# Even attention of a two-block kernel: three projection chunks change places, eight more attention units run beside the chunks, and products of the output projection stand between the last units

## What is computed

```python
proj = h @ w_in                       # 1024 x 3080: qa ka va | qb kb vb | forget gates
# differential attention, 4 heads of 2 maps each, chunk mask and ALiBi
s_a = qa . ka * scale - slope * dist  ;  p_a = softmax(s_a)
o_a = (p_a[0] - lam * p_a[1]) @ va    ;  o_a = rms_norm(o_a) * subln_g * 0.8
# forgetting attention, 8 heads, causal
s_b = qb . kb * scale + cq - cum_f    ;  o_b = softmax(s_b) @ vb
mix = concat(o_a, o_b) @ w_out        # 1024 x 1024
h = layer_norm(ALPHA * h + mix)       # then the feed-forward part
```

## Time and profile before

| | |
|---|---|
| median of 3 runs | 1156.41 us (1154.87 to 2162.7) |
| the profiled execution | 1158.03 us, span 1156.2 us |
| TensorE busy, mean granted clock | 1117.0 us (97%), 0.982 |
| VectorE, ScalarE, GpSimd busy | 778.5, 623.9, 332.9 us |
| HBM | 153 GB/s over the span |

### The profile page before, as it was taken

How to read it: one execution, slowest core, us unless ns; L and a number is a source line. 1 busy time by engine, 2 the same in 40 slices (tenths; PEclk the granted TensorE clock), 3 DMA queues, 4 the chain that set the end, 5 groups by cost and what they waited for, 6 DMA issues and landing times.

```text
span 1156.2 us, 24136 instructions
## 1 busy us (share of the span) xinstructions
PE 1117.0 (97%) x8917; PEld 1063.4 (92%) x8917; DVE 778.5 (67%) x1404; ACT 623.9 (54%) x1194; POOL 332.9 (29%) x371
## 2 busy tenths in 40 slices
PE   6998989999988999999999999999999999999997
PEld 6976989999988888779999999999979999999996
DVE  5766578887467777736888555495556567887454
ACT  5657555556445646754665543474335645665343
POOL 3002323334201101125466312100013334666130
PEclk9999999999999999959999999999999999999999
DMA  6573436675555533204555554655422655555651
GB/s 195 135 207 111 111 104 187 184 201 164 168 194 196 182 96 94 91 1 147 182 170 166 178 178 163 212 193 182 145 73 91 202 182 182 183 181 181 203 182 53
DMA packets 202489, 180.61 MB, mean 156 GB/s; under 512 B 6800, under 2 KB 200755, under 8 KB 202163
## 3 DMA queue, kind: packets, MB, share of 16 engines
q1 hardware_dynamic: 201907, 175.74, 48.8%
q0 software_dynamic: 512, 3.94, 0.9%
HBM read 176.28 MB, written 1.05 MB: 153 GB/s over the span
## 4 chain that ended last, share of the span: by engine, by line
PE 84%; DVE 5%; ACT 4%; issue 2%; DMA 2%; POOL 2%; SPq 0%; ACTq 0%; DVEq 0%; POOLq 0%
PE ps L1925 24%; PE ps L1926 24%; PE ps L1927 24%; DVE wlo L1297 2%; PE ps L2338 2%; PE ps L2468 2%; ACT whi L759 1%; PE ps L2083 1%; POOL acc L589 1%; DMA raw<-even_w_in 1%; PE ps L2295 1%; PE ps L2320 1%; PE ps L2446 1%; PE ps L2294 1%; DVE h L1534 1%
## 5 line engine op out<-in xcount | busy, mean ns | idle before, releaser
L1297 DVE TENSOR_TENSOR wlo<-raw,whi 128x1024 fp32r<-128x1024 f32 x316 | 394.8, 1286 | 161.5 <-ACT whi L759 159.8
L759 ACT ACTIVATE whi<-raw 128x1024 fp32r<-128x1024 f32 x316 | 318.1, 1051 | 170.4 <-PE ps L1927 156.9
L1925 PE MATMUL ps<-xh,whi 128*128 128x256 f32 (+1 forms) x880 | 251.9, 286 | 4.4 <-issue 2.1
L1926 PE MATMUL ps<-xl,whi 128*128 128x256 f32 (+1 forms) x880 | 249.8, 284 | 0.0
L1927 PE MATMUL ps<-xh,wlo 128*128 128x256 f32 (+1 forms) x880 | 249.6, 284 | 0.0
L1925 PE MATMUL ps<-xrh,whi 128*128 128x274 f32 (+2 forms) x832 | 242.3, 291 | 3.4 <-DVE wlo L1297 3.3
L1927 PE MATMUL ps<-xrh,wlo 128*128 128x274 f32 (+2 forms) x832 | 238.5, 287 | 0.0
L1926 PE MATMUL ps<-xrl,whi 128*128 128x274 f32 (+2 forms) x832 | 238.5, 287 | 0.0
L1925 PE MATMUL ps<-fh,whi 128*128 128x256 f32 (+1 forms) x688 | 194.1, 282 | 2.2 <-DVE wlo L1297 2.2
L1927 PE MATMUL ps<-fh,wlo 128*128 128x256 f32 (+1 forms) x688 | 194.0, 282 | 0.0
L1926 PE MATMUL ps<-fl,whi 128*128 128x256 f32 (+1 forms) x688 | 193.9, 282 | 0.0
(11 more groups left out here) (356 smaller groups left out, 1598.6 us busy)
## 6 DMA issues: line engine op xcount, KB each, us to landing
raw<-ffn_w SPq DMA_DIRECT2D x128, 512.0 KB, 4.4
raw<-ret_w_in SPq DMA_DIRECT2D x48, 512.0 KB, 4.5
raw<-even_w_in SPq DMA_DIRECT2D x24, 512.0 KB, 4.7
raw<-w_ffn_gate SPq DMA_DIRECT2D x22, 512.0 KB, 4.0
raw<-w_ffn_up SPq DMA_DIRECT2D x22, 512.0 KB, 5.2
raw<-w_ffn_down SPq DMA_DIRECT2D x16, 512.0 KB, 4.4
raw<-ret_w_out SPq DMA_DIRECT2D x16, 512.0 KB, 4.2
raw<-w_in SPq DMA_DIRECT2D x12, 512.0 KB, 5.4
```

The lines of the kernel that those rows point to most:

```text
L759: A(whi[:, slot, s * 1024:s * 1024 + 1024], raw[:, slot, s * 1024:s * 1024 + 1024], ACT.Copy).then_inc(w_hi_ready, 1)
L1297: V.tensor_tensor(wlo[:, slot, s * 1024:s * 1024 + 1024], raw[:, slot, s * 1024:s * 1024 + 1024], f32(whi[:, slot, s * 1024:s * 1024 + 102 ...
L1925: T.matmul(dst, w[0], x[0], start=first, stop=False)
L1926: T.matmul(dst, w[0], x[1], start=False, stop=False)
```

## The change

- `EVEN_COLS`: the eight chunks beside the units now hold, in order, differential values 0 and 1, forget queries 0, forget keys 0, forget values 0, forget queries 1, forget keys 1, forget values 1. `qk_high`, `qk_low` and `twice` follow it.
- The chunks have 4, 4, 6, 6, 5, 5, 5 and 4 steps beside them: 39, so `ALONE` = 39.
- The alone steps' scores are one unit ahead in two banks, as in the steps beside chunks, and all value products go to banks 6 and 7. So the transposes of step i wait for the copy of the value product of step i-1 (`u_out`, o-1).
- The four norm products stand at steps 31, 32, 33, 33 (`NORM_AT`), in banks 2 and 3; TensorE waits before chunk 7 until ScalarE has read the last (`oarstd` 4). The scores of unit 36, in step 35, wait for the keys of chunk 6 (`qk_ready` 16), which are taken out right before.
- `even_mix(j, k)` is one k-tile of chunk j of the output projection, six matmuls. In steps 39 to 44 stand (0,0) to (0,5), in steps 46 to 48 (1,0) to (1,2), each between scores and transposes (`OUT_AT`). After step 52 come (1,3), (1,4), (1,5), (0,6), (0,7), (1,6), (1,7); chunks 2 and 3 are as before.
- The second chunk of `even_out` is split between the units: ScalarE's halves in steps 41 and 43, VectorE's in 42 and 44 (before: after step 52).
- GpSimd makes high and low part of each head in one go, and those of `of` 0 and 1 after them; the high part of `of` 2 is made by ScalarE in step 51, and the low parts of 2 and 3 by VectorE after step 52.

```diff
+WITH_UNITS = (4, 4, 6, 6, 5, 5, 5, 4)
+VALUE_CHUNKS = (0, 1, 4, 7)
+FORGET_QK = {2: (0, 0), 3: (1, 0), 5: (0, 1), 6: (1, 1)}
+EVEN_COLS = [0, 256, 512, 768, 1024, 1280, 1536, 2048, 2560, 1792, 2304, 2816]
+NORM_AT = (31, 32, 33, 33)
+OUT_AT = {ALONE + n: (0, n) for n in range(6)}
+OUT_AT.update({ALONE + 7 + n: (1, n) for n in range(3)})
+OUT_LEFT = [(1, k) for k in range(3, 6)]
+OUT_HI_AT, OUT_LO_AT = (ALONE + 2, ALONE + 4), (ALONE + 3, ALONE + 5)
...
-    return 4 + i % 2 if i < ALONE else (4 + ALONE % 2, 5 - ALONE % 2, 0)[(i - ALONE) % 3]
+    return 4 + i % 2
...
-            def even_unit(i):
-                ahead = LEAD[i >= ALONE]
+            def even_unit(i, between=None):
...
-                if i + ahead < len(UNITS):
-                    scores(i + ahead)
+                if i + 1 < len(UNITS):
+                    scores(i + 1)
+                if between is not None:
+                    between()
...
-                    wait(pe, u_out if out_bank(o - 2)[0] == 6 + o % 2 else u_pT, o - 1)
+                    wait(pe, u_out, o - 1)
...
+                if c == 7:
+                    pe.wait_ge(oarstd, 4)
...
+            def even_mix(j, k):
+                c = C0["even_out"] + j
+                pe.wait_ge(w_lo_ready, 2 * c + 1 + k // 4)
+                pe.wait_ge(oa_lo, k + 1) if k < 4 else pe.wait_ge(u_flo, k - 3)
+                for dst, col, m in pair("even_out", j, N2):
+                    ins = three(dst, tile(c % 2, 256 * k + col, m), [v[:, k, ALL] for v in rows_x], k == 0, k == KD - 1)
+                if k == KD - 1:
+                    ins.then_inc(mm_done, 1)
...
-                even_unit(i)
+                even_unit(i, (lambda: even_mix(*OUT_AT[i])) if i in OUT_AT else None)
+            for j, k in OUT_LEFT + [(j, k) for j in range(2) for k in (6, 7)]:
+                even_mix(j, k)
```

More of the change, by code:

```diff
@@ L649, in _, with twice @@
             ins.then_inc(sel_ready, 1)
-            def twice(i):
-                for n in range(4):
+            def twice(i, pairs):
+                for n in pairs:
                     s0 = 8 * i + 2 * n
-                    pool.wait_ge(qk_hi, 8 * i + n + 1)
+                    pool.wait_ge(qk_hi, 8 * i + n + 1 + (2 if i == 1 and n >= 2 else 0))
                     if n == 0:
-                        if not is_first(i):
+                        if i > 0:
                             pool.wait_ge(q_twice, 8 * i)
@@ L672, in _ @@
                 nc.gpsimd.tensor_tensor(oasq[:, hd, :], oa[:, hd, :], oa[:, hd, :], ALU.mult).then_inc(oasq_ready, 1)
[L674 to L679, removed]
+            pool.wait_ge(oasq_ready, 4)
+            twice(1, (2, 3))
+            pool.wait_ge(q_twice, 16)
             for hd in range(4):
@@ L685, in _ @@
                 nc.gpsimd.tensor_copy(xh[:, 4 + k, :], of[:, k, :]).then_inc(u_fhi, 1)
[L686 to L690, removed]
+                pool.wait_ge(u_fhi, k + 1)
+                nc.gpsimd.tensor_tensor(xl[:, 4 + k, :], of[:, k, :], f32(xh[:, 4 + k, :]), ALU.subtract).then_inc(u_flo, 1)
             def hidden(base, cols, hi, lo):
@@ L1761, in _ @@
                     even_value_tiles(7)
-            split_at(C0["even_out"] + 1)
+                if i in OUT_LO_AT:
+                    split_at(C0["even_out"] + 1, (OUT_LO_AT.index(i),))
+            dve.wait_ge(u_flo, 2)
+            for k in (2, 3):
+                dve.wait_ge(u_fhi, k + 1)
+                V.tensor_tensor(xl[:, 4 + k, :], of[:, k, :], f32(xh[:, 4 + k, :]), ALU.subtract).then_inc(u_flo, 1)
             def layer_var(n, j, cols, between=None):
@@ L2339, in even_unit @@
                     ins.then_inc(u_pv, 1)
-                hd = i - NORM - 1
-                if 0 <= hd < 4:
+                for hd in norm_heads(i):
                     pe.wait_ge(oasq_ready, hd + 1)
                     if hd == 0:
-                        pe.wait_ge(ve_ready, 9)
-                    wait(pe, oarstd, hd)
-                    T.matmul(ps[1][:, 0:N2], ones[:, :], oasq[:, hd, :], start=True, stop=True).then_inc(oastat, 1)
+                        pe.wait_ge(qk_ready, 14)
+                    wait(pe, oarstd, hd - 1)
+                    T.matmul(ps[2 + hd % 2][:, 0:N2], ones[:, :], oasq[:, hd, :], start=True, stop=True).then_inc(oastat, 1)
             def even_value_turn(c):
@@ L2377, in _ @@
                     even_value_turn(7)
-                even_unit(i)
-            pe.wait_ge(u_max, len(UNITS))
-            pe.wait_ge(oarstd, 4)
-            def even_mix(k):
-                pe.wait_ge(oa_lo, k + 1) if k < 4 else pe.wait_ge(u_flo, k - 3)
-            for j in range(4):
-                wait(pe, tile_ready, TILES[S_LN] + 2 * (j - 1) if j >= 2 else 0)
-                product(C0["even_out"] + j, (C0["even_out"] + j) % 2, pair("even_out", j, N2), rows_x, ALL, 256,
-                        ready=even_mix if j == 0 else None).then_inc(mm_done, 1)
+                even_unit(i, (lambda: even_mix(*OUT_AT[i])) if i in OUT_AT else None)
+            for j, k in OUT_LEFT + [(j, k) for j in range(2) for k in (6, 7)]:
+                even_mix(j, k)
+            for j in (2, 3):
+                pe.wait_ge(tile_ready, TILES[S_LN] + 2 * (j - 1))
+                product(C0["even_out"] + j, (C0["even_out"] + j) % 2, pair("even_out", j, N2), rows_x, ALL, 256).then_inc(mm_done, 1)
             def raw(cols):
```

100 lines of the change are left out of this document (52 added, 48 removed).

## The result

| | |
|---|---|
| after, median of 13 executions | 1163.1 us (1160.57 to 1169.19) |
| before, beside it | 1156.93 us |
| ratio | 1.0058, 95% interval [1.0042, 1.0073] |
| the profiled execution of after | 1169.19 us, span 1167.4 us, mean granted clock 0.977 |

The forecast was 1153.8 us, range 1148 to 1161: outside the range, and on the other side of the kernel before. One execution of the kernel before took 2162.7 us; the ratio leaves it out.

A forecast was written before the change was run, and what follows sets the result against it. TensorE's stream was taken to bound the kernel up to output chunk 0, then a loop of other engines. Its end 3.2 us earlier, less 0.6 for half clock, gave 2.6 us off 1156.4: 1153.8 us, range 1148 to 1161.

The forecast's parts named there:

- What bounds the kernel: TensorE's own stream up to the first output chunk, then a 25.0 us loop round VectorE, ScalarE and GpSimd to `stat`.
- X: End of output chunk 0, when its y can start: 523.75 before, 520.5 forecast; bringing it forward brings `stat` forward.
- Part 1: Steps 31 to 38 move beside chunks 2 to 7, where they and the norm products take 11.0 us.
- the factor 0.75: Steps 31 to 38 get cheaper beside chunks by this ratio: 11.3 us becomes 8.5 us.
- Part 2: Waits of the new order ahead of step 39: 1.5 us, bounds 0 and 4; moved steps end at 492.1.
- the 0.7 for all other chunks: Waits beside chunks apart from the 0.8 us stall for chunk 6's keys, completing a total of 1.5 us.
- Part 3: Steps 39 to 52 run at full clock with nine k-tiles added: 24.4 us, step 52 ending at 516.5.
- A: Half clock returns in the tail around steps 48 to 52: 2.9 us more, 1156; 0.2 together with another case.
- B: Alone steps from step 39 on never keep the clock: 37.8 us, X 12 us later, 1168; chance 0.07.
- Part 4: Output chunks: X 3.2 us earlier; a 3.1 us TensorE gap ahead of chunk 2, half clock behind it costing 0.6.
- C: VectorE or ScalarE late in every chunk, stalls 4 us and more, steps 31 to 38 no cheaper: 1159; chance 0.11.
- D: Every wait met and transposes in alone steps as cheap as beside chunks: gain 8 us at most, 1148; chance 0.12.

The follow-up runs named there:

- e3: Changed kernel with no output-projection product between units, all sixteen k-tiles after step 52, chunk 0 first: 1164.20 us, ratio 1.0062 to the kernel before.
- e4: Changed kernel with only the order of the last seven k-tiles changed, output chunk 0 finished after one tile of chunk 1: 1159.92 us, ratio 1.0038.
- e8: Kernel before plus six wide matmuls on fixed data, results unused, in each of steps 39 to 48: 1166.34 us, ratio 1.0045.
- e9: Changed kernel with chunk 6's keys copied out earlier, output chunk 0 first after step 52, last value products in banks 4 and 5: 1155.87 us, ratio 1.0001.
- e10: e9 with the steps spread 4, 4, 5, 5, 5, 5, 6, 5 and norm products one step earlier: 1156.19 us, ratio 0.9994.
- e12: Changed kernel with chunk 6's keys early, last value products in banks 4 and 5, six chunk 1 products in steps 46 to 51: 1157.33 us, ratio 1.0008.
- e1: Changed kernel run again unaltered, to profile another execution: 1162.83 us, ratio 1.0050 to the kernel before.
- e2: Changed kernel with ScalarE copying chunk 6's keys out in step 34, before the copy of the transposes: 1161.28 us, ratio 1.0038.
- e5: Changed kernel with 4, 4, 5, 5, 5, 5, 6, 5 steps beside the chunks and norm products one step earlier: ratio 1.0027.
- e7: Kernel before's chunk order, 31 steps beside chunks and norms, with the changed kernel's nine products between units, scores one ahead: 1167.02 us, ratio 1.0055.

## Why the prediction was wrong

**What bounds the kernel: right.** X to `stat` was 25.0 us before and in e3, e4, e8, e9 and e10, and 25.2 to 25.4 in the eight traces with a half-clock run behind the gap. e4 moved X alone, and the end followed in its trace; e12 moved it the other way.

**Part 1: not far off, and not tested by itself.** Step 39 was late by 4.1 us in e1. By distances from start to start, against the same shapes without a wait, some 5 us of lateness lie ahead of step 39 in e1 and some 0.5 in the kernel before. The 4.5 us added are 3 more than the forecast's 1.5. The 1 us that is left can be in this part, the factor 0.75 or the breaks of the stream, and no run separates them.

**Part 2 failed: the new order adds some 4.5 us of waits where I took 1.5 with a bound of 4.** Step 39 starts at 495.87 in e1, at full clock, and a start after 495 was one of the forecast's own signs of being wrong. 3.7 us in e1 are listed as waits, 3.2 more than before; the rest is small lateness that hides in modelled ends. The keys of chunk 6 cost 1.3 listed (0.8 forecast): the duration of the copy was right, its place on ScalarE, behind a whole step, was not looked at. Take it out and 1.2 us come back (e2). The larger error is the 0.7 for all other chunks. It rested on a mean: 0.5 us idle in 78.74, and VectorE busy 75%, to rise to 80%. In e1 VectorE was busy for 65.26 of 94.12 us, 69%: its mean share fell, and the waits came all the same. A mean says nothing of five or six steps that share a chunk with a block of 1.6 + 1.8 us of copies. These 3 us take the forecast gain of 3.2 us at X away; with the other 1 us ahead of step 39 and 0.6 behind it e1 has a loss of 1.5 there. e2 and e9 take the keys' share away and get it back; e5 shows that the other share moves elsewhere when the steps are spread.

**Part 3: right at full clock, wrong in taking it for granted.** 24.9 us for 24.4 forecast in e1, 30.4 in the execution first profiled, where 508 to 523 is at half clock. Rivals A and B were each put as all or nothing. The truth is between: the same program keeps the clock between step 39 and X in one profile (e1) and loses it for 14 us there in the other, and the time is a median over such executions. The forecast counted the removal of all 27.3 us at half clock of the kernel before. The typical execution has only 16 less, so 11 us at a third of a us each, nearly 4 us, are missing.

**Part 4: right.** The gap of 3.1 us was listed as 3.2, with 3.4 us at half clock behind it; it cost 0.2 to 0.4 us of `stat`, 0.6 forecast.

**The rivals.** None fits by its number. C comes nearest in kind, with stalls of 4 us and more, and put 1159. B's mechanism shows in e7. D's terms add up to 8.6 us, not 8.

**The base.** The gain was taken off the median of the runs shown, although it was summed against one execution 1.6 us above it. e9 shows what that is worth: its profiled X is 2.5 us earlier than in the profiled kernel before, its span 2.1 us less, and its median is equal. Where the clock varies between executions, one profile is one draw from them.

**Where the expected gain went**, then, with the medians: keeping the clock is worth 5 us; the change pays about 11 at equal clock. Some 4.5 of these are Part 2's waits. The steps after 39 have no slack left once the clock is kept (23.10 of 23.31 us busy in e9), so a product placed there isn't free: it costs 0.9 us by the forecast's own price, which the 24.9 us bear out. Six of chunk 1's stand ahead of X in the changed kernel, where before they lay behind it, inside the 25.0 us that other engines fill; 5.4 us. The forecast had counted these products in its sum for X, so they are a cost of the change and not one of its misses. That these two make up nearly all of the 11 is argued, not shown. The second is tested by e4, which takes two such products from ahead of X and brings it forward by 1.5 us, and by e12.

**Open.** What decides within one program whether the clock holds was not settled. e7 and e8 began their wide work as the clock was falling; wide work begun in step 31, without the moved steps, was not tried. Nor was a finer cut of the copies in chunks 3 and 4.

## What to carry to other kernels

Price a denser interleave by the chunk in which the longest block of a helper engine falls: put that block, copies and splits together, against the time between two steps, not a mean share against 100%. Where another loop sets the end, keep work that isn't ahead of its start out of the stream before it, however idle that stream looks at a low clock; once the clock is kept, it isn't idle. And where the granted clock is part of the gain, read it over many executions, since one profile shows one of the outcomes.

## What the hardware showed that was not expected

- One program has two outcomes with nothing in the 7 to 9 us between them (e7: 1155.4 to 1157.3 and 1166.8 to 1171.4 us; e8 likewise), with mean granted clocks of 0.985 to 0.989 and 0.972 to 0.977. In the profiled execution of the slower group the clock falls at 493.3 us; the faster group has no profile.
- In four of five traces the clock fell behind a wait of 1.32 us in a dense stream (first profile: 486.50, then 0.22 us a matmul from 488.5 to 492), in the fifth not. It also fell in thin stretches in which TensorE is listed as busy throughout (before: 21.68 of 21.68 us from 493.25).
- An idle gap of 1.89 us in the first block, the same in all 14 traces, has half clock behind it in five; one of 3.2 us ahead of chunk 2 has it in eight of eight, one of 1.7 us there in none of three.
- Wide matmuls inside a lost stretch didn't restore the clock while the thin work went on: 41 us at half clock in e7 with nine products of six in it. In the stream of chunk 2, unbroken, it was back after 3.4 us.
- Within the executions of one version a us at half clock goes with 0.2 to 0.45 us of time, by version.
